# State-space outputs in double groups, attention in mirrored rounds, GpSimd copies half of the compression rows, pages ahead of weights

## The reference, cut to what matters

```python
u, q, kv6, nsa_gates, merge_logits = split(rmsnorm(x) @ w_in)
# branch A: complex diagonal state space model, 32 groups of 16 channels, then a gated linear unit
y = real(C @ scan(lam_bar, B @ u)) + d * u
ssm_out = gelu(y) * sigmoid(gelu(y) @ w_glu + b_glu)
# branch B: sparse attention, 8 heads over 2 key/value heads
kcmp = gelu(flat(k_blocks + pe_k) @ w_cmpk1) @ w_cmpk2     # blocks of 64 rows, compressed
vcmp = gelu(flat(v_blocks + pe_v) @ w_cmpv1) @ w_cmpv2
o = g0 * attend(q, kcmp, vcmp) + g1 * attend(q, selected blocks) + g2 * attend(q, window)
x = x + rmsnorm((gate0 * (ssm_out @ w_br_ssm) + gate1 * (o @ w_br_nsa)) @ w_out)
# then cross-attention into 256 memory tokens and a squared-ReLU MLP
```

## Time and profile before

| | |
|---|---|
| median of 3 runs | 1180.26 us (1179.4 to 1180.98) |
| profiled execution, its time | 1182.53 us |
| profiled execution, its span | 1180.9 us |
| granted TensorE clock, mean | 0.987 of full speed |
| PE busy | 1127.6 us |
| DVE, ACT, POOL busy | 654.4, 476.7, 168.5 us |
| whole-array fp32 products of the later stages (L1519, L1773, L1443, not touched) | 297.0, 195.1 and 41.2 us |

### The profile page before, as it was taken

One profiled execution on the slowest core, in us unless ns is written; L12 is line 12 of the kernel. 1 busy time (PEld: TensorE's weight loads), 2 busy tenths in 40 slices (PEclk: granted clock), 3 DMA queues, 4 the chain that ended last, 5 costly groups with the idle time before them and its releaser, 6 DMA issues.

```text
span 1180.9 us, 21973 instructions
## 1 busy us (share of the span) xinstructions
PE 1127.6 (95%) x8474; PEld 1008.7 (85%) x8474; DVE 654.4 (55%) x1153; ACT 476.7 (40%) x762; POOL 168.5 (14%) x281
## 2 busy tenths in 40 slices
PE   6999999999999998899999989999999999999997
PEld 5888787778777676799887978899999989999997
DVE  4467992765765423562535567456442345666663
ACT  3100220455775414341323576453432334655550
POOL 1020024835303222000000030001000000001100
PEclk9999999998999999999999999999999999999998
DMA  7791254734728548364556426742532232232201
GB/s 200 171 241 54 82 183 134 190 111 120 178 63 276 160 144 284 103 206 129 206 148 220 159 82 204 251 143 72 176 122 96 74 99 79 72 107 72 72 1 76
DMA packets 167105, 164.21 MB, mean 139 GB/s; under 512 B 41573, under 2 KB 148034, under 8 KB 166874
## 3 DMA queue, kind: packets, MB, share of 16 engines
q1 hardware_dynamic: 157658, 134.84, 38.1%
q0 software_dynamic: 9344, 27.98, 7.9%
HBM read 154.21 MB, written 12.73 MB: 141 GB/s over the span
## 4 chain that ended last, share of the span: by engine, by line
PE 79%; DVE 6%; SPq 5%; ACT 4%; issue 4%; DMA 1%; POOL 0%; DVEq 0%; ACTq 0%
PE banks L1519 22%; PE banks L1773 15%; PE banks L1017 14%; PE banks L1473 4%; PE banks L1235 4%; SPq L658 2%; PE banks L1443 1%; PE banks L1023 1%; PE banks L1347 1%; DVE rounded L2826 1%; PE banks L1287 1%; SPq L707 1%; PE banks L1270 1%; SPq L678 1%; PE banks L1298 1%
## 5 line engine op out<-in xcount | busy, mean ns | idle before, releaser
L1519 PE MATMUL banks<-rounded 128*128 128x288 f32 (+1 forms) x2304 | 297.0, 289 | 4.0 <-DVE rounded L2941 3.4
L1519 PEld LDWEIGHTS banks<-rounded 128*128 128x128 f32 x2304 | 291.4, 188 | 7.6 <-DVE rounded L2941 4.1
L1017 PE MATMUL banks<-arena 128*128 128x256 f32 (+1 forms) x896 | 209.2, 393 | 2.3 <-issue 1.8
L1017 PEld LDWEIGHTS banks<-arena 128*128 128x128 f32 x896 | 168.8, 190 | 36.3 <-issue 1.9
L1773 PE MATMUL banks<-rounded 128*128 128x272 f32 x1536 | 195.1, 290 | 3.8 <-DVE rounded L3123 3.8
L1773 PEld LDWEIGHTS banks<-rounded 128*128 128x128 f32 x1536 | 194.5, 190 | 4.5 <-issue 3.1
L2826 DVE TENSOR_TENSOR rounded<-arena,rounded 128x2048 fp32r<-128x2048 f32 x59 | 137.0, 2321 | 68.4 <-ACT rounded L1989 68.3
L1989 ACT ACTIVATE rounded<-arena 128x2048 fp32r<-128x2048 f32 x59 | 112.5, 1907 | 22.4 <-PE banks L1443 8.9
L3123 DVE TENSOR_TENSOR rounded<-arena,rounded 128x1088 fp32r<-128x1088 f32 x64 | 82.9, 1304 | 60.2 <-ACT rounded L2254 60.2
L2254 ACT ACTIVATE rounded<-arena 128x1088 fp32r<-128x1088 f32 x64 | 71.1, 1114 | 81.0 <-PE banks L1773 79.8
L2095 ACT ACTIVATE arena<-banks 128x256 f32<-128x256 f32 (+1 forms) x64 | 25.5, 398 | 126.3 <-PE banks L1519 126.3
(11 more groups left out here) (438 smaller groups left out, 1473.6 us busy)
## 6 DMA issues: line engine op xcount, KB each, us to landing
arena<-in_w_up SPq DMA_DIRECT2D x22, 1024.0 KB, 5.5
arena<-in_w_down SPq DMA_DIRECT2D x16, 1024.0 KB, 5.2
arena<-in_w_in SPq DMA_DIRECT2D x13, 1024.0 KB, 10.3
upper<-in_cache_nsa_kv SPq DMA_DIRECT2D x64, 128.0 KB, 2.5
upper<-in_cache_nsa_kv POOLq DMA_DIRECT2D x64, 128.0 KB, 4.8
arena<-in_w_out SPq DMA_DIRECT2D x8, 1024.0 KB, 7.0
arena<-in_cache_mem_kv SPq DMA_DIRECT2D x16, 512.0 KB, 7.1
arena<-in_cache_nsa_kv SPq DMA_DIRECT2D x90, 64.0 KB, 2.3
```

The costliest lines, as they stand in the source:

```text
L1017: ins = mm(bank(b + h, (NA, NB)[h], rows=M), lhsT(k), rhs[:, k, toks], start=(k == 0), stop=(k == K - 1))
L1519: ins = mm(bank(b, N), w[:, k], a[:, k, toks], start=(k == 0 and z == 0), stop=(k == K - 1 and z == 2))
```

## The change

PE forms the state-space outputs for two quarters at once: a step has four Toeplitz products and eight state products, over four banks. The eight result banks are all different (`Y_BANK`). The transposes of the result and the GLU products are put between the last steps. The six 32-row transposes of L1165 come together behind the other transposes.

In attention PE's list is written for two pairs at a time: scores, values, transposes, compression, transposes, values, scores, so that the scores that end one round stand next to those that begin the following one. `cmp1` comes in pieces of 16 steps (8 and 8 at a unit's start). The block scores are in two parts, at pairs 11 and 19. The last product `gates((0,))` is cut in two parts.

POOL, not ACT, copies half 1 of tiles 4 to 15, in its queue ahead of the pages of tile `j+5`. DVE, not POOL, zeroes the blocks of `w1`. In SP's queue the pages of tile 4 go ahead of the second half of the key weights, and the pages of tiles 11 and 12 ahead of the first half of the value weights.

```diff
-        YT_BANK = (4, 5, 0, 1)
+        YT_BANK = (4, 5, 6, 7)
+        Y_BANK = (4, 5, 6, 7, 2, 3, 0, 1)
...
-        CMP_STEP = (0, 10, 21, 32, 40, 48, 56, 64)
-        SC_AT = 10
-        assert PAIRS[SC_AT][0] == 0
+        BLOCK_ROWS = {11: (0, 1), 19: (2, 3)}
+        SC_AT = 18
+        assert all(PAIRS[i][0] == 0 for i in BLOCK_ROWS)
         RELAY_AT = {}
         for _u in range(1, CU):
             for _k in range(4):
-                RELAY_AT.setdefault((0, 8 * _u - 5 + _k), []).append(4 * _u + _k)
-                RELAY_AT.setdefault((1, 8 * _u + (0, 0, 1, 2)[_k]), []).append(4 * _u + _k)
+                RELAY_AT.setdefault((0, 8 * _u - 4 + _k), []).append(4 * _u + _k)
...
+                if n == 4:
                     sp.wait_ge(sem("yT_T"), 8)
                     compress_weights(0, 1)
...
-                if j in (10, 12):
-                    sp.wait_ge(sem("cmp_done"), 3 + (j == 12))
-                    compress_weights(1, int(j == 12))
+                if j == 12:
+                    for part in range(2):
+                        sp.wait_ge(sem("cmp_done"), 3 + part)
+                        compress_weights(1, part)
...
-            def zero_blocks(part, name):
-
-                pool.memset(w1[part][0:64, :, 64:P], 0.0)
-                signal(pool.memset(w1[part][64:P, :, 0:64], 0.0), name)
-
             known.update(known_pages(pool, (4, 5), SP_PAGES, PAGES))
             for n, j in enumerate(RAW_ORDER):
+                if j >= 9:
+                    relay(pool, pool.tensor_copy, j - 5, 1)
                 raw_pages(pool, j, known, SP_PAGES, PAGES, f"more_rows_in_{raw_slot(j)}")
                 if n == 3:
-                    pool.wait_ge(sem("y_mm"), 8)
-                    zero_blocks(0, "w1a_zeroed")
                     pool.wait_ge(*step("ssm_states"))
                     store(pool, ssm_prompt[0, 0].rearrange("(g m) s z -> g (m s z)", m=2), hout[0:GP, 0:256])
                     store(pool, ssm_sample[0].rearrange("b (g m) s z -> (b g) (m s z)", m=2), hout[:, 256:512])
-                    pool.wait_ge(sem("yT_T"), 8)
-                    zero_blocks(1, "w1b_zeroed")
                 if j in (8, 9):
                     known.update(known_pages(pool, (j - 2,), SP_PAGES, PAGES))
+            for j in range(4 * CU - 5, 4 * CU):
+                relay(pool, pool.tensor_copy, j, 1)
             for gg in range(NG2):
...
                 for t in range(4):
-                    pe.transpose(bank(4 + i % 2, P, t * P), s[:, t, :], ident)
+                    ins = pe.transpose(bank(4 + i % 2, P, t * P), s[:, t, :], ident)
+                signal(ins, "qk_T")
+            for i, s in enumerate(srcs):
                 ins = pe.transpose(bank(7, TS, i * TS), s[0:TS, 4, :], ident[0:TS, 0:TS])
-                signal(ins, "qk_T")
+            signal(ins, "qk_T")
...
+            def y_terms(qs, i):
+
+                outs = [(q * 4 + i, m, bank(Y_BANK[2 * q + m], P, i * P, rows=YROWS)) for q in qs for m in range(2)]
+                for gp, m, out in outs:
+                    g = 2 * gp + m
+                    mm(out, UT[:, g, 0:YROWS], Tz[:, :, g * C_SSM:(g + 1) * C_SSM], start=True, stop=False)
+                for z in range(2):
+                    for gp, m, out in outs:
+                        ins = mm(out, Z[m * 64:m * 64 + 64, z, gp, 0:YROWS], M2[m * 64:m * 64 + 64, z, gp],
+                                 start=False, stop=(z == 1))
+                        if i == 3 and z == 1:
+                            signal(ins, "y_mm")
+
...
+            for i in range(4):
+                y_terms((0, 1), i)
+            pe.wait_ge(sem("lin_out"), done_unit(("gate", 11)))
+            y_terms((2, 3), 0)
+            y_terms((2, 3), 1)
+            pe.wait_ge(sem("y_out"), 1)
+            pe.wait_ge(*step("hfin_ready"))
+            for z in range(2):
+                pe.transpose(bank(4, P, z * P, rows=GP), hfp[:, z], ident)
+            for z in range(2):
+                ins = pe.transpose(bank(4, P, 256 + z * P), hfs[:, z], ident)
+            signal(ins, "hfin_T")
+            y_terms((2, 3), 2)
+            y_rows_T(0)
+            y_rows_T(1)
+            y_terms((2, 3), 3)
+            y_rows_T(2)
+            y_rows_T(3)
+            glu_rows(0, 0)
+            glu_rows(0, 1)
+            y_rows_T(4)
+            y_rows_T(5)
+            glu_rows(1, 0)
+            glu_rows(1, 1)
+            y_rows_T(6)
+            y_rows_T(7)
+            for k in range(2, 4):
+                for m in range(2):
+                    glu_rows(m, k)
+            for m in range(2, 4):
+                for k in range(4):
+                    glu_rows(m, k)
...
+            def block_scores(i):
+
+                pe.wait_ge(sem("cmp_out"), 1)
+                pe.wait_ge(sem("p_ready"), 2 * (i - 1))
+                for q in BLOCK_ROWS[i]:
+                    for r in range(REP):
+                        mm(bank(2, 16, 256 + (q * REP + r) * 16), qT[:, r, q * P:(q + 1) * P], kc_bd, start=True, stop=True)
 
...
+            def pair_T(j):
+
+                qt = PAIRS[j][0]
+                if (j + 2) % 8 == 0 and j > 0:
+                    pe.wait_ge(sem("cmp_out"), (j + 2) // 8)
+                pe.wait_ge(sem("p_scaled"), j + 1)
+                if j >= 1:
+                    pe.wait_ge(sem("pT_ready"), j)
+                for g in range(2):
+                    for kt in range(qt + 1):
+                        ins = pe.transpose(bank(4 + g, P, kt * P), p_sb[:, j % 2, g, kt * P:(kt + 1) * P], ident)
+                signal(ins, "p_T")
+
...
+            pair_scores(0)
+            pair_scores(1)
+            cmp1(0, 0, 16)
+            for e in range(2, NPAIR, 2):
+                u, k = e // 8, e % 8
+                pair_scores(e)
+                if e >= 4:
+                    pair_values(e - 3)
+                if k == 0:
+                    cmp2(u - 1)
+                    cmp1(u, 0, 8)
+                pair_T(e - 2)
+                cmp1(u, 8 * k if k else 8, 8 * k + 16)
+                pair_T(e - 1)
+                if e + 1 in BLOCK_ROWS:
+                    block_scores(e + 1)
+                pair_values(e - 2)
+                pair_scores(e + 1)
+            pair_values(NPAIR - 3)
...
-                for j in RELAY_AT.get((1, i), ()):
-                    relay(act, lambda o, a: fn(o, a, ACT.Copy), j, 1)
...
+            for part, name in enumerate(("w1a_zeroed", "w1b_zeroed")):
+                dve.wait_ge(*((sem("yT_T"), 8) if part else (sem("y_mm"), 8)))
+                own(dve.memset(w1[part][0:64, :, 64:P], 0.0))
+                ins = dve.memset(w1[part][64:P, :, 0:64], 0.0)
+                own.wait()
+                signal(ins, name)
...
+                if i % 2 == 0:
+                    pair_max(i)
+                    if i % 8 == 0 and i:
+                        cmp_take(i // 8 - 1)
+                if i >= 1:
+                    pair_scale(i - 1)
+                if i % 2 == 0 and i >= 4:
+                    pair_out(i - 3, i - 2)
+                if i % 2:
+                    pair_max(i)
```

301 lines of the change are left out of this document (145 added, 156 removed).

## The result

| | before | changed |
|---|---|---|
| median | 1180.95 us (1179.4 to 1183.81, 5 runs) | 1190.22 us (1187.78 to 1192.9, 5 runs) |
| profiled execution: time, span | 1182.53, 1180.9 us | 1191.84, 1189.9 us |
| end of the last state-space product | 213.29 us | 211.46 us |
| first scores of attention | 232.23 us | 230.00 us |
| first piece of unit 2 | 308.50 us | 313.50 us |

The changed kernel is slower: the ratio to before is 1.0075, 95% interval 1.0056 to 1.0094. The forecast was 1178.3, 1171 to 1183.5. The lower rows show where it went: 1.8 us were won in the state-space outputs, unit 2 began 5.0 late, and the stretch from there to the sample attention took 90.7 us instead of 83.2.

What follows compares the result with a forecast made beforehand. PE was taken to bound the kernel, busy 1127.6 of 1180.9 us. Unit 2's earlier start -2.6, slow clock +2.0 and unit 2 to sample products -1.4 sum to -2.0: 1178.3 us against the median, range 1171 to 1183.5.

Steps and rivals of the forecast that it cites:

- The cost of a change of kind: PE pays at each change between whole array, row halves and column halves: 0.15 us in the outputs, 0.17 in attention.
- the state-space outputs: State-space stage on PE: 32 runs become 16, -2.4 us; with transposes moved ahead, the last product comes 1.65 earlier.
- That PE would wait at unit 2 for SP: Compression unit 2: PE ready at 298 waits 6 to 8 us for value weights, begins at 305.9, not 308.50: -2.6.
- The 18 pages at 9.0: SP's queue: 18 more page transfers ahead of the value weights take 0.5 us each, putting the weights' issue at 299.2.
- SP is 1.65 earlier all along: SP's queue: the 1.65 us won in the state-space outputs is subtracted from the value weights' issue time.
- That ahead of unit 2 only the weights gate: Before unit 2: all PE gains there are hidden behind its wait for the value weights, which land at about 306.
- rival B: Unit 2: weights do not gate, PE begins at 298, 10.5 us earlier, without wait or slow clock; 1168.4 us; chance 0.10.
- The restart, +2.0: Behind the wait at unit 2 PE may be granted half clock again: +2.0 us, ends 0 and 3.4.
- DVE's zeroing at nothing: DVE instead of POOL zeroes four blocks, some 7.2 us more for DVE; counted at nothing, any loss hidden before unit 2.
- "DVE works beside POOL's copies": Unit 2 to sample products: one reason for new PE waits, together taken as +1.0 us, ends 0 and 4.6.
- Rival C: POOL's copies ahead of the pages from tile 9 on hold up cache pages; slower, up to 1188 us; chance 0.17.
- R: Time of one POOL copy of 128x1024, taken as 2 us; it decides from 3.4, the gain is gone at 3.65.

Runs made afterwards that it cites:

- e2: Changed kernel, but SP loads the second half of the key weights and the small weights ahead of tile 4's pages, as before; 1190.47 us, ratio 1.0082.
- e3: Changed kernel, but SP issues the value weights as before, first half behind tile 10, second behind tile 12; 1183.07 us, ratio 1.0031.
- e4: Changed kernel with the edits of e1, e2 and e3 together: ACT copies half 1, SP's queue in the order of before; 1183.94 us, ratio 1.0025.
- e10: e4 with ACT's copies one to a pair instead of two at pair 8u; 1177.45 us, ratio 0.9959.
- e11: e10 with POOL loading nine pages and SP seven of tiles 9, 10 and 11; 1175.32 us, ratio 0.9947.
- e8: e4 with one page of 16 moved from SP to POOL in each tile (8 and 8); 1184.0 us, ratio 1.0022.
- e1: Changed kernel, but ACT again copies half 1 of tiles 4 to 15 and POOL copies nothing; 1189.8 us, ratio 1.0088.
- e5: e3 with each of POOL's copies of tiles 4 to 15 cut in four instructions; 1179.2 us, ratio 0.9982.
- e6: e3, but ACT copies tiles 14 and 15, at pairs 25 and 27, and POOL only 12 and 13 of the last four; 1186.68 us, ratio 1.0037.
- e12: e5 with POOL loading nine pages and SP seven of tiles 9, 10 and 11; 1185.17 us, ratio 1.0039.
- e7: Kernel before, with only POOL instead of ACT copying half 1 of tiles 4 to 15, ahead of tile j+5's pages; 1189.84 us, ratio 1.0064.
- e9: Kernel before, with only both halves of the value weights moved behind the pages of tile 12; 1183.17 us, ratio 1.0022.

## Why the prediction was wrong, step by step

**The cost of a change of kind, and the state-space outputs: right.** PE's timeline in the outputs:

```profile
209.46 1.04 PE L1178 MATMUL banks<-upper,arena 128*72 128x128 f32 x8
210.43 1.10 PE L1181 MATMUL banks<-upper,arena 64*72 64x128 f32 x16
211.46 0.72 PE L1196 MATMUL banks<-arena,upper 72*128 72x72 f32 x8
```

A double step takes 2.00 (forecast 2.1) and the last product ends 1.8 earlier (forecast 1.65).

**That PE would wait at unit 2 for SP: right in kind, wrong in size.** PE was ready at 301.5 (298 forecast; it had lost 5.3 and a restart at unit 1, which nothing in the forecast had) and went on at 313.5 (305.9 forecast). Of the 7.6, 5.8 are the issue at 305.04 and not 299.2. The 18 pages at 9.0 were right: from tile 9's start to the weights it is 29.3, and the 20.1 between those places before plus 9.0 is 29.1. What failed is the start of the sum, that SP is 1.65 earlier all along. It was 4.0 later: tile 9 starts at 275.76, before at 271.72. Most of the 4.0 is this execution's, in the stall behind the key weights; the five other kernels with the same order start tile 9 at 271.85 to 272.78. But the 1.65 is lost in all of them, and in e2 too, which has the order of before: there the first key weights go out 2.3 earlier (211.14 against 213.43), and tile 9 starts at 271.84. The head start goes in the issue of the transfers; the first two of the key weights take 4.00 in e2, before 2.45. The other 1.8 are the landing: with both halves issued together it was 8.5 from issue to use.

**That ahead of unit 2 only the weights gate: wrong in e3, e4 and e10.** With the weights out of the way the pages of tile 11 are next, at 304.3 to 306.3. I had given 298 as PE's own pace and rival B's time. There was no B to be had in any run: unit 2 waits for SP unless SP issues fewer transfers, and even then it began at 301.88 (e11). The start of unit 2 before, 308.50, was 4.2 above the lowest of these floors, so all that PE gained ahead of unit 2 could bring 4 at most. This is the step that a reader should take from the trace first: follow the other queue to its own earliest time.

**The restart, +2.0: measured 2.8.** Inside the ends given. One reading in that paragraph is wrong: the slow stretch before does not lie behind the block scores. They start at 275.10 and take 5.12, and the clock falls at 277.21, within them.

**DVE's zeroing at nothing: right.** Unit 0 begins at 231.92 without a wait. It holds while the first pages are early; in e8 they are not, and PE waits.

**"DVE works beside POOL's copies", +1.0 with an upper end of 4.6 for all waits: this is the step that failed.** The one wait for the scaling is 6.2 and brings 2.7 more of slow clock, 8.9 together. From 83.16: 4.6 less for changes of kind, 2.2 more for what was moved in, 1.7 less for waits of before that are gone, 6.8 of waits, 2.8 and 2.7 of slow clock. That is 91.4; 90.66 were measured, so the gain from the list of PE was as forecast or a little more. I had the hint in the earlier trace rows, a DVE copy of 2.62 beside POOL and 1.03 alone, and read it as a slower copy. It fits a copy that waited for the end of POOL's instruction: the memset ends at 217.82 and the copy 0.80 later, much as the one at 351.24 ends 0.93 behind POOL's. Without POOL's copies the term is still too small. In e11 PE waits 3.7 in this stretch, 2.0 more than before, and the stretch takes 85.75, where the forecast, with its restart, had 83.8.

**Rival C, POOL's copies hold up the pages: wrong for the changed kernel.** R is 2.0, as I took it (by the rule of the Trainium skill's page GPSIMD Engine Reference, section "Performance pitfalls for Q7 kernels", it would have been an estimate of 2.5, and by its other figure, 1.9 cycles, one of 1.6; the measured 2.0 lies between the two; 2.5 would have taken the margin to 3.4 from 1.4 to 0.9, which is less than halving it). PE never waits there for POOL. The loss on POOL's side came by the other road: not what POOL is late with, but whom it stops. The same page of the Trainium skill, section "Specifications", says that GpSimd shares its interfaces to SBUF with VectorE, and that it contends with VectorE's instructions in a two-port mode or with two inputs from SBUF. The multiplication has two such inputs, and agrees. That the scaling and the copies, with one input, ran in a two-port mode, no row here shows. The rows add that DVE's operation stands until POOL's whole instruction has ended: 1.76 for 0.16.

**After the sample attention begins** 12.5 us late, 3.4 are given back. Before has two stretches of half clock in the sample attention (near 397 and 462), the changed kernel one (near 435), which is 1.6; and the wait for the pages of the second group is 2.64 before and 1.07 in the changed kernel, where they had more time, 1.6 more. This was only read in the two traces.

**What each part costs or brings, by the runs.** Times against before, in us: the start of unit 2 (308.50) and the first sample product (391.66) in the one profiled execution of each kernel, and the median in its series.

| | unit 2 begins | first sample product | median |
|---|---|---|---|
| changed | +5.0 | +12.5 | +9.3 |
| e1, copies on ACT | +1.8 | +7.5 | +9.1 |
| e2, key weights as before | +2.8 | +9.5 | +9.8 |
| e3, value weights as before | -4.2 | +2.1 | +2.4 |
| e4, all three undone | -3.1 | +0.4 | +3.3 |
| e5, e3 and copies in pieces | -2.3 | +1.4 | -2.4 |
| e6, e3 and two copies on ACT | -1.1 | +8.3 | +5.1 |
| e8, e4 and a page to POOL | -1.4 | +3.9 | +2.4 |
| e10, e4 and ACT spread | -3.3 | -0.3 | -4.0 |
| e11, e10 and fewer pages on SP | -6.6 | -4.0 | -6.1 |
| e12, e5 and fewer pages on SP | +1.7 | +5.6 | +3.7 |
| e7, before and POOL's copies | +3.7 | +11.0 | +8.3 |
| e9, before and late value weights | +2.4 | +4.0 | +1.7 |

Behind the first sample product no kernel is edited, and yet the profiled executions take from 782.0 to 789.7 there. So a trace shows where a wait stands, and what a kernel costs as a whole is told by the medians.

POOL's copies: 8.3 on the kernel before (e7). The order of the value weights: 7 on the changed kernel (e3), 1.7 on before (e9). The order at the key weights: nothing that can be measured (e2). PE's new list with ACT's old copies: nothing (e4); with the copies spread, 4.0 faster than before (e10); with fewer pages on SP, 6.1 (e11). That the changes do not add (e1 brought nothing, e3 seven) fits what the traces show, that a wait taken away uncovers the next one; no run tests it by itself. What stays open is why the stall behind the key weights differs between executions, and how much of the scatter of the changed kernel's and e6's runs is due to it; where most of e10's gain over e4 lies; and when DVE gets in between two pieces of POOL's.

## What to carry to other kernels

Before crediting an engine with an earlier arrival, walk the queue that feeds it to its own earliest time: here the gain ahead of unit 2 was capped at 4 us by SP's page transfers, and more was had only by taking transfers off SP. A copy moved to GpSimd can hold VectorE until the GpSimd instruction ends; here it held multiplications, scalings and copies from SBUF to SBUF, for up to 2.3 us each. So look at which engine's short operations stand on the path, and don't let several GpSimd copies stand in a row beside them. Shorter GpSimd instructions helped (e5), but not at every place. Spreading ACT's copies over its list gave more than moving them away.
